# A ninth place for down weights in layer 2 of a two-layer mixture-of-experts kernel

## What is computed

```python
def hier_moe(h, ...):
    ...
    y = jnp.zeros(h.shape, h.dtype)
    for g in range(N_GROUPS):
        sl = slice(g * EXPERTS_PER_GROUP, (g + 1) * EXPERTS_PER_GROUP)
        a = jnp.einsum('btd,edf->btef', h, w_gate[sl])
        u = jnp.einsum('btd,edf->btef', h, w_up[sl])
        hid = jax.nn.silu(a) * u * combine[:, :, g, :, None]
        y = y + jnp.einsum('btef,efd->btd', hid, w_down[sl])
    return y
...
xl_new = xl_new + g2_l * hier_moe(h2, ...)      # the residual
```

## Time and profile before

| | |
|---|---|
| median of 3 runs | 1494.05 us (1492.22 to 1494.19) |
| span of the profiled execution | 1490.7 us |
| so what lies around the span, taken against the median | 3.35 us |
| PE busy | 1395.0 us (94%) |
| DVE, ACT, POOL busy | 779.2, 367.0, 177.2 us |
| HBM read | 346.57 MB |

### The profile page before, as it was taken

How to read it: one execution, slowest core, us unless ns; L and a number is a source line. 1 busy time by engine, 2 the same in 40 slices (tenths; PEclk the granted TensorE clock), 3 DMA queues, 4 the chain that set the end, 5 groups by cost and what they waited for, 6 DMA issues and landing times.

```text
span 1490.7 us, 19015 instructions
## 1 busy us (share of the span) xinstructions
PE 1395.0 (94%) x7438; PEld 803.7 (54%) x7438; DVE 779.2 (52%) x1710; ACT 367.0 (25%) x801; POOL 177.2 (12%) x118
## 2 busy tenths in 40 slices
PE   6999999999989999989997778999999999999786
PEld 3444444554444445665554447744678876665453
DVE  2579944568886963433211117894853444444232
ACT  4112314432223012222222124141543203000001
POOL 0021421000011210012221210151000110000000
PEclk9999999999999999999999999999999999999998
DMA  9312130144434347289999988232523488999995
GB/s 386 150 41 107 57 113 0 57 155 167 173 102 194 125 197 312 87 338 417 419 419 420 420 336 355 92 113 101 203 92 141 170 321 332 402 420 420 421 419 215
DMA packets 59692, 350.76 MB, mean 235 GB/s; under 512 B 8404, under 2 KB 15060, under 8 KB 28112
## 3 DMA queue, kind: packets, MB, share of 16 engines
q1 hardware_dynamic: 54000, 338.99, 57.3%
q0 software_dynamic: 5024, 8.40, 1.5%
q10 hardware_dynamic: 576, 2.10, 0.3%
HBM read 346.57 MB, written 11.80 MB: 240 GB/s over the span
## 4 chain that ended last, share of the span: by engine, by line
PE 77%; DMA 11%; SPq 4%; DVE 4%; ACT 2%; issue 1%; DVEq 0%; POOLq 0%; ACTq 0%
PE bank L432 73%; DMA arena<-w_up_in 10%; SPq L2826 3%; ACT arena L1261 2%; PE bank L778 2%; SPq L2835 1%; DMA arena<-glu_in 1%; PE bank L532 1%; DVE arena L1722 1%; PE bank L1146 1%; DVE arena L2110 1%; DMA x<-x_in 0%; DVE am L2008 0%; DVE arena L2107 0%; PE bank L1166 0%
## 5 line engine op out<-in xcount | busy, mean ns | idle before, releaser
L432 PE MATMUL bank<-arena 128*128 128x512 f32 (+10 forms) x6000 | 1245.3, 446 | 48.5 <-DMA arena<-w_up_in 38.8
L432 PEld LDWEIGHTS bank<-arena 128*128 128x128 f32 (+4 forms) x6000 | 668.5, 161 | 529.7 <-issue 406.0
L1261 ACT ACTIVATE arena<-bank 128x512 f32<-128x512 f32 (+5 forms) x425 | 202.6, 497 | 921.9 <-PE bank L432 813.2
L1722 DVE SCALAR_TENSOR_TENSOR arena<-arena,bank 64x256 f32<-64x256 f32 (+2 forms) x121 | 57.8, 479 | 301.4 <-ACT arena L1261 227.4
L1722 DVE SCALAR_TENSOR_TENSOR arena<-arena,vec 128x512 f32<-128x512 f32 (+1 forms) x254 | 177.5, 771 | 0.4
L2008 DVE TENSOR_REDUCE am<-bank 128x1 f32<-128x512 f32 (+1 forms) x96 | 55.5, 599 | 130.9 <-PE bank L432 130.7
L2635 POOL TENSOR_TENSOR arena<-arena 128x512 f32<-128x512 f32 (+1 forms) x32 | 39.2, 1225 | 442.6 <-DVE arena L1722 442.6
L1261 ACT ACTIVATE arena<-bank,am 128x512 f32<-128x512 f32 (+1 forms) x96 | 58.6, 613 | 89.9 <-DVE am L2011 89.7
L2674 POOL DMA_INDIRECT y<-arena,routing x33 | 33.0, 999 | 183.8 <-ACT arena L1261 183.8
L778 PEld LDWEIGHTS bank<-con,arena 128*128 128x128 f32 x240 | 29.6, 141 | 38.2 <-issue 21.4
L778 PE MATMUL bank<-con,arena 128*128 128x128 f32 x240 | 38.7, 276 | 7.2 <-DVE arena L2023 4.7
(11 more groups left out here) (205 smaller groups left out, 792.0 us busy)
## 6 DMA issues: line engine op xcount, KB each, us to landing
arena<-w_gate_in SPq DMA_DIRECT2D x61, 1024.0 KB
arena<-w_up_in SPq DMA_DIRECT2D x61, 1024.0 KB
arena<-w_down_in SPq DMA_DIRECT2D x52, 1024.0 KB, 16.5
arena<-mg_in SPq DMA_DIRECT2D x12, 2048.0 KB, 7.9
arena<-adaT_in SPq DMA_DIRECT2D x40, 512.0 KB, 3.7
arena<-adaT_in SPq DMA_DIRECT2D x16, 1024.0 KB, 7.5
arena<-ada_in SPq DMA_DIRECT2D x6, 2048.0 KB, 16.4
arena<-mo_in SPq DMA_DIRECT2D x6, 2048.0 KB, 7.9
```

What stands on the lines that cost most here:

```text
L432: return nc.tensor.matmul(out, w, rhs, start=start, stop=stop)
L1261: return nc.scalar.activation(out, in_, fn, **kw)
L1722: return V.scalar_tensor_tensor(out, in0, sc, in1, op0=op0, op1=op1)
```

## The change

The two latent tiles `x[:, 2:4]` become a ninth place for down weights in layer 2. `NDOWN[1]` goes from 8 to 9, so expert e goes to place e mod 9, and the wait of `expert_wd(e)` names the block of expert e − 9 where it named that of e − 8. The first load into the new place is that of expert 8. No earlier expert was there, and it waits for `comb_full` to reach 2, which is when block 0 has been combined. Its place in SP's order stays the same. A ninth semaphore `wd_ready` is needed, for which four semaphores of the first microseconds are merged into two (`silc_tanh` with `lam_exps`, `silc_ready` with `lam_sums`), and a name that nothing used is dropped (`rows_ready`).

```diff
-NDOWN = (7, 8)
+NDOWN = (7, 9)
...
-                               (down_more, 18672, 10240, 4096, x[:, 0:2, :].rearrange("p t d -> p (t d)"), 16384, 8192, 6144))[l]])
+                               (down_more, 18672, 10240, 4096, x[:, 0:2, :].rearrange("p t d -> p (t d)"), 16384, 8192, 6144,
+                                  x[:, 2:4, :].rearrange("p t d -> p (t d)")))[l]])
...
-        lam_sums, lam_exps = sem("lam_sums"), sem("lam_exps")
+        act_early, dve_early = sem("silc_tanh_lam_exps"), sem("silc_ready_lam_sums")
...
                 def expert_wd(e):
                     j = down_slot(l, e)
+                    if l == 1 and e == NDOWN[1] - 1:
+                        sp.wait_ge(s["comb_full"], 2)
                     if e >= NDOWN[l]:
                         sp.wait_ge(s["y_full"], e - NDOWN[0] + 1 if l == 0 else (e - NDOWN[1]) // 2 + 1)
                     sp.dma_start(wd[j], a["w_down"][l, e]).then_inc(wd_ready[j], 16)
```

More of the change, by code:

```diff
@@ L210, in build @@
         half_ready = [sem(f"ada_half_ready{b}") for b in range(2)]
-        silc_tanh, silc_ready = sem("silc_tanh"), sem("silc_ready")
         dve_step, pool_step = sem("dve_step"), sem("pool_step")
@@ L227, in build @@
         ONLY0 = ("xg_ready0", "xg_ready1", "y_stored0", "y_stored1", "yg_ready0", "yg_ready1", "yg_ready2", "yg_ready3", "ov_xg", "ov_stored")
-        ONLY1 = ("slot_ready", "rows_ready", "pick_ready", "spread_ready", "comb_full", "ov_rows", "ov_step")
+        ONLY1 = ("slot_ready", "pick_ready", "spread_ready", "comb_full", "ov_rows", "ov_step")
         both = {n: sem(n) for n in LAYER0}
@@ L547, in _ @@
             pe.wait_ge(consts_set, 2)
-            pe.wait_ge(silc_ready, 1)
+            pe.wait_ge(dve_early, 1)
             turn_x(0, "n1", 0, 0, xs[:, 0, :])
@@ L1318, in _ @@
             act.wait_ge(cvec_loaded, 16)
-            f(silc[:, 0:16], silc[:, 16:32], ACT.Tanh, scale=0.5).then_inc(silc_tanh, 1)
+            f(silc[:, 0:16], silc[:, 16:32], ACT.Tanh, scale=0.5).then_inc(act_early, 1)
             act.wait_ge(consts_set, 2)
@@ L1362, in _ @@
                 if l == 0:
-                    act.wait_ge(lam_sums, 1)
-                    f(small[:, 5:9], small[:, 1:5], ACT.Exp).then_inc(lam_exps, 1)
+                    act.wait_ge(dve_early, 2)
+                    f(small[:, 5:9], small[:, 1:5], ACT.Exp).then_inc(act_early, 1)
                 else:
@@ L1813, in _ @@
             V.memset(small[:, 0:1], EPS).then_inc(consts_set, 1)
-            dve.wait_ge(silc_tanh, 1)
+            dve.wait_ge(act_early, 1)
             step(stt(silc[:, 0:16], silc[:, 0:16], 1.0, silc[:, 16:32], ADD, MUL))
             V.tensor_scalar(silz.rearrange("p (k n) -> p k n", k=KD)[:, :, 0:2], silc[:, 0:16].rearrange("p (k n) -> p k n", k=KD),
-                            0.5, None, MUL).then_inc(silc_ready, 1)
+                            0.5, None, MUL).then_inc(dve_early, 1)
             dve.wait_ge(S[0]["ms_ready"], 4)
@@ L1861, in _ @@
                     if (l, m) == (1, 1):
-                        ins.then_inc(lam_sums, 1)
+                        ins.then_inc(dve_early, 1)
                     else:
                         step(ins)
-            dve.wait_ge(lam_exps, 1)
+            dve.wait_ge(act_early, 2)
             for l in range(DEPTH):
```

## The result

The changed kernel takes 1499.91 us (median of 6 runs, 1498.15 to 1501.52) against 1494.01 us for the kernel before (6 runs, 1491.15 to 1497.75). The ratio is 1.0043 with a 95% interval of 1.0031 to 1.0055, so it is slower by 0.43%, which is 6.4 us, by the ratio, and by 5.9 us between the two medians. (The ratios of this document are those on record with their intervals and need not be the quotient of the two medians beside them.) Forecast were 1500.4 us, a range of 1497.5 to 1503.0 us, and a chance of 0.87 for slower.

What follows compares the result with a forecast made beforehand. The stream of expert weight loads in layer 2 was taken to bound the end. With 6.4 us of empty stream and other terms at 0, 1494.05 + 6.4 gave 1500.4 us, range 1497.5 to 1503.0 us.

Steps and rivals of the forecast that it cites:

- The bound: Layer 2's experts: one stream of transfers from 1276.76 us sets the end; each microsecond it runs empty reaches the end.
- The new wait: SP issues expert 8's down load after block 0's combination, at 1293.06 us instead of 1284.06 us, 9.0 us later.
- The hole: Transfers run dry at 1288.33 us and are back, in effect, at 1294.73 us: 6.4 us, reaching the end; chance 0.80.
- the restart: After expert 8's late load is issued, the emptied transfer stream needs 1.67 us to be back in effect.
- The lower bound of 4.7 us: Least cost at expert 8's load: stream empty from 1288.33 to 1293.06 us, no time added for getting going again.
- a lucky tail: TensorE's work after the last landing varies with granted clock, about 1.7 us either way; 1.3 us taken off the low end.
- The ninth place is worth nothing: Layer 2's down loads: the extra place gives nothing back, since transfers had queued work at each wait; costed at 0.
- The shrunken waits: SP's waits at layer 2's down loads, 35.2 us in 6 waits before, mostly go; named as a sign of being right.
- What was said of TensorE: Its first wait for a load comes before block 7, some 3 us long, ending at about 1357 us.
- The covered hole: Rival: TensorE bounds the end and the stream has 6.4 us of reserve, so no change, 1494 us; chance 0.07.
- the ninth place pays: Rival: stream starves at SP's waits for down places, so one MiB in advance gains 2.5 us, about 1491.5 us; chance 0.05.
- The larger slowdown: Rival: TensorE waits longer in blocks 7 to 15, clock lower more often, whole 9.0 us passes, about 1503 us; chance 0.08.

Runs made afterwards that it cites:

- experiment 3: Changed kernel with expert 8's down load waiting for comb_full 4 in place of 2, one block more: 1510.64 us, ratio 1.0123 to the kernel before.
- experiment 4: Changed kernel with expert 8's down load waiting only for TensorE's last residual matmul, not the end of the combination: 1497.48 us, ratio 1.0026 to the kernel before.
- Experiment 5: Changed kernel, wait on the residual's own end, residual matmuls moved ahead of block 0's down products: 1493.53 us, ratio 1.0001 to the kernel before.
- experiment 1: Changed kernel with expert 8's down load and its wait issued behind expert 9's down load and both experts' gate and up loads: 1493.03 us, ratio 0.9999.
- experiment 8: Kernel before with the merged semaphores alone, eight places and no wait for comb_full: 1492.25 us against 1492.96 us, ratio 0.9995.
- experiment 2: Kernel before, still eight places, with only the added wait of expert 8's down load for comb_full at 2: 1499.89 us, ratio 1.0043.
- experiment 11: Changed kernel, expert 8's down load behind expert 9's gate and up loads, down loads 26 to 31 behind their own pair's gate and up loads: 1488.98 us, ratio 0.9962.

## Why the prediction held, step by step

**The bound.** That the stream of transfers sets the end was right. Experiments 3 and 4 show it as a line with slope one: 11.0 us more of delay gave 11.0 us of stream, and 1.9 us less gave 2.0 us less, without any reserve. Experiment 5 shows the flat part, where the load is issued before the queue is dry.

**The new wait.** Predicted was the issue at 1293.06 us, or 16.30 us after gu6. Measured were 16.29 us.

**The hole.** Predicted 6.4 us, measured 6.0 us in the stream's length and 5.9 us in the medians. The size was nearly right, but a step behind it was muddled. I added 1.67 us for the restart and named the cost of the restart as an unknown, with 4.7 us for a hole without any. It isn't a term at all. The same restart stands at the start of the stream, behind gu6's issue, so it moves the moment at which the queue runs dry as much as the moment at which it is full again. Windows of the changed kernel, from 0.30 to 8.00 us behind the issue of gu6 and behind that of expert 8's load, show that the two are alike:

```profile
1276.80:1284.50 7.70, 7.32 (x77) 5.40 (x78) 5.30 (x13) 0.68 (x2) 0.00 (x0) 1.00 0.93 355
1293.09:1300.79 7.70, 7.70 (x96) 5.45 (x98) 2.99 (x9) 0.60 (x1) 0.00 (x0) 1.00 0.93 353
```

Over 7.70 us these rates are 2.73 and 2.72 MB, or 6.46 and 6.43 us at 423 GB/s, which puts the effective start 1.54 and 1.57 us behind the issue.

What is left is the distance of the two issues less the work in between, 16.29 − 9.92 = 6.4 us, however long the restart is, as long as it is the same at both places. So the weighing of the Trainium skill's first byte of 600 ns (page "DMA: Bandwidth & Descriptors", section "Latency and other measured facts") against my 1.67 us was idle: put in at both places, that figure would give an estimate of 6.4 us too, not 5.3. The lower bound of 4.7 us had no ground either, and the 1.3 us of a lucky tail that went into the low end of the range were never derived: the prediction's own figure for that luck was 1.7 us. The 0.4 us that are missing to the measured 6.0 are not explained. Lengths of the stream that should be equal (before, and experiments 1, 5 and 8) lie between 179.2 and 179.6 us, which is about as much, and the kernel before has the longest of them. Against their mean of 179.4 us the changed kernel's stream is 6.2 us longer.

**The ninth place is worth nothing.** Right, and shown from three sides: with the hole and without the place (experiment 2), with the place and without the hole (1), and with a shorter tail (11). But the way there had a step that was read wrongly. The prediction says that of SP's 35.2 us of waits for down places most goes, since every even expert's load waits for one block less. With the place and without the hole 26.7 us remain beside the new wait (experiment 1), for the odd expert's load right behind waits for the same block as before. In the changed kernel 12.2 us remain beside it, but the hole without the place also leaves only 17.0 us (experiment 2). The shrunken waits that the prediction named as a sign of being right did show, mostly for another reason. The forecast doesn't rest on this step, for it had put the gain at 0.

**What was said of TensorE.** Its first wait for a load came in front of block 7 and was 2.64 us long; the products behind it start at 1356.32 us. Forecast were about 1357 us and some 3 us. The tail brought neither good nor bad luck here: the 72 rows after the chain's last landing took 7.26 us before and 7.25 us after the change.

**The merged semaphores** cost nothing, as costed (experiment 8).

**The rivals.** The covered hole fell with experiment 3, since even 17 us of hole came through whole. That the ninth place pays fell with experiments 1 and 11. The larger slowdown would have needed the full 9.0 us, and 6.0 us came. The other half of that rival did show, without an effect on the end: from 1400 to 1450 us the granted clock was 0.93 after and 0.97 before, and TensorE waited for loads once more, but what the chain did behind its last landing took the same time.

## What to carry to other kernels

When transfers in one stream set the end, ask of a change only whether the stream runs dry. A wait in a queue that works in order cost here the time since the stream's first issue, with nothing issued after the four loads, less the transfer time of those loads; it cost nothing when the same load stood a few places further back. One more buffer was worth what could be loaded into it before the stream began, measured here as 2.2 us of stream for one MiB, and a buffer that came free only after that was worth nothing. A shorter total of waits in the queue that issues the loads is no sign of a gain: here most of the drop came where the transfers had fallen behind. Then look at the order: a load that the end waits for should not have loads ahead of it that are needed later, which gave 0.2 to 0.3% here with no memory at all.

## What was not expected of the hardware

What is queued seems to show in SP's own rows. While little is queued, the issue of one load of 1 MiB takes SP some 0.4 us. From about 1337 us on most take 2.1 us, here in the kernel before:

```profile
1336.81 2.13 SPq L2826 DMA_DIRECT2D arena<-w_gate_in  x1
1338.97 2.12 SPq L2826 DMA_DIRECT2D arena<-w_up_in  x1
```

I read this as SP being held back until earlier transfers have moved; no run here tests it. The load of the chain lands 27.7 us after it was started, which at 0.42 MB per us is an estimate of 11 MiB. Where the transfers are behind by the hole, the long issues begin sooner, with and without the ninth place: at 1324.81 us in the changed kernel and at 1328.80 us in experiment 2, both 48 us after gu6, where it is 60 us before and in experiment 1 (1337.22 us). That fits the shorter waits for places behind a hole. In the second half of the stage SP would then be held by what is queued and hardly by places. From 1345 us on the kernel before has a single wait at a down load:

```profile
SPq L2835 <- PE bank L432: 6.6, 1, 6.6
```

SP's rows show no pause of that length there but an issue under way, from 1370.20 us for 7.85 us, so what it waited for is open.
